# Half-granule signals for the weights' low parts, with three edits to ScalarE's side work and one to a product's order

## What is computed

```
for layer in range(2):                       # hybrid_layer
    p = split_columns(rmsnorm(x, norm_g) @ w_in)
    hm = mlstm_chunkwise(conv+silu(q, k), v, gates)      # 4 heads
    hg = gla_chunked(q, k, v, decays)                    # 4 heads, then rmsnorm by head
    hd = dsa_sparse_attention(q, k, v, index scores, top 128)
    x = x + concat(y_ml, y_gla, y_dsa) @ w_out
u = rmsnorm(x) @ w_in_2                      # second_block
y_a = rwkv7_branch(u)                        # forward and backward scan
y_b = diff_attn_branch(u)                    # 4 heads, 2 softmaxes each
x = x + (gate_a * y_a + gate_b * y_b) @ w_out_2
x = x + relu(rmsnorm(x) @ w_ff1)**2 @ w_ff2
x = x + sigmoid(rmsnorm(x) @ w_ple_gate) * (p @ w_ple_proj)
out = rmsnorm(x)
```

## Time and profile before

| | |
|---|---|
| median of three runs | 2360.22 us |
| the profiled execution's own time | 2368.48 us |
| its span, first to last instruction | 2366.7 us |
| PE busy | 2259.0 us, 95% of the span |
| DVE, ACT, POOL busy | 1202.9, 947.8, 899.2 us |
| idle time of PE that ended with POOL's low part (L346) | 28.5 us in 12 waits |
| granted TensorE clock, mean | 0.987 of 2.4 GHz |

### The profile page before, as it was taken

The page is one execution under the profiler, slowest core; times in us unless marked ns, Lnnn a source line. Parts: engine busy times, 40 slices in busy tenths (PEclk is TensorE's granted clock), DMA queues, the critical chain, the costliest instruction groups (busy, mean ns, idle before and its releaser), DMA issues. The chain is left out here.

```text
span 2366.7 us, 38426 instructions
## 1 busy us (share of the span) xinstructions
PE 2259.0 (95%) x16046; PEld 1750.6 (74%) x16046; DVE 1202.9 (51%) x2014; ACT 947.8 (40%) x1364; POOL 899.2 (38%) x674
## 2 busy tenths in 40 slices
PE   7999999999999999999999988888999999999997
PEld 5776777787877857777778777776666778888885
DVE  5544843334246467343343878853544667307334
ACT  5433355345253224654343433324266333212243
POOL 3342243334443404333344432222332445545543
PEclk9999999999999999999999999998999999999998
DMA  4221222222322212212233200002221233222332
GB/s 148 86 89 36 72 81 71 72 72 76 101 83 78 67 45 85 85 63 80 64 102 104 75 3 4 4 13 83 67 67 54 80 98 98 96 95 94 98 98 71
DMA packets 50568, 175.18 MB, mean 74 GB/s; under 512 B 6036, under 2 KB 7004, under 8 KB 50396
## 3 DMA queue, kind: packets, MB, share of 16 engines
q1 hardware_dynamic: 50396, 172.73, 22.5%
HBM read 170.60 MB, written 2.11 MB: 73 GB/s over the span
## 5 line engine op out<-in xcount | busy, mean ns | idle before, releaser
L346 POOL TENSOR_TENSOR w_low<-work,w_high 128x512 fp32r<-128x512 f32 x614 | 826.5, 1367 | 1215.4 <-ACT w_high L295 1215.4
L276 PE MATMUL ps<-x_high_tiles,w_high 128*128 128x512 f32 x1544 | 626.1, 406 | 28.4 <-POOL w_low L346 20.9
L295 ACT ACTIVATE w_high<-work 128x1024 fp32r<-128x1024 f32 x307 | 325.0, 1058 | 733.8 <-PE ps L276 730.7
L276 PE MATMUL ps<-x_low_tiles,w_high 128*128 128x512 f32 x1544 | 605.1, 392 | 0.8 <-DVE x_low_tiles L369 0.8
L276 PE MATMUL ps<-x_high_tiles,w_low 128*128 128x512 f32 x1544 | 604.6, 392 | 0.0
L276 PE MATMUL ps<-arena_parts,w_high 128*128 128x512 f32 x1264 | 399.7, 393 | 11.3 <-POOL w_low L346 7.2
L276 PEld LDWEIGHTS ps<-x_high_tiles,w_high 128*128 128x128 f32 x1544 | 291.4, 189 | 132.6 <-issue 42.4
L276 PEld LDWEIGHTS ps<-x_low_tiles,w_high 128*128 128x128 f32 x1544 | 291.5, 189 | 64.5 <-DVE x_low_tiles L369 1.6
L276 PEld LDWEIGHTS ps<-x_high_tiles,w_low 128*128 128x128 f32 x1544 | 291.8, 189 | 62.7 <-issue 6.0
L276 PEld LDWEIGHTS ps<-arena_parts,w_high 128*128 128x128 f32 x1264 | 238.8, 189 | 64.3 <-POOL w_low L346 8.6
L276 PE MATMUL ps<-arena_parts,w_low 128*128 128x512 f32 x608 | 237.6, 391 | 0.0
(11 more groups left out here) (454 smaller groups left out, 2903.9 us busy)
## 6 DMA issues: line engine op xcount, KB each, us to landing
work<-w_first SPq DMA_DIRECT2D x178, 512.0 KB, 3.7
work<-w_second SPq DMA_DIRECT2D x134, 512.0 KB, 3.7
xT_sb<-xT SPq DMA_DIRECT2D x8, 256.0 KB, 7.6
outT<-arena SPq DMA_DIRECT2D x8, 256.0 KB, 2.1
arena<-distance_bias SPq DMA_DIRECT2D x4, 256.0 KB
small<-small SPq DMA_DIRECT2D x1, 815.5 KB, 4.6
arena<-consts SPq DMA_DIRECT2D x1, 544.0 KB, 3.7
base<-consts SPq DMA_DIRECT2D x1, 512.0 KB
```

The costliest lines, as they stand in the source:

```text
L276: ins = pe.matmul(out, lhsT, rhs, start=(n == 0 and k == 0 and q == 0), stop=(n == unit["granules"] - 1 and k == len(ops[i]) - 1 and q == 2))
L295: act.activation(m.wh[:, split_of(g), :], m.raw[:, raw_of(g), :], ACT.Copy).then_inc(sem["high_ready"], 1)
L346: ins = pool.tensor_tensor(m.wl[:, split_of(g), part], m.raw[:, raw_of(g), part], m.wh[:, split_of(g), part].bitcast(F32), ALU.subtract)
```

## The change

1. POOL raises `low_ready` after each of its two instructions for a granule instead of after the second alone. PE waits for the first count at the granule's start, and once more before the first tile of the second half of each job's tiles (`second`). SP's waits are for the same events as before, with doubled counts.
2. `renormalise_side`: the high part of the eighth tile is made in the same turn as the other seven.
3. `gla_side`: the four exponentials come one turn after the logarithms.
4. `rwkv_keys_side`: three of the six exponentials come in one turn and three in the next, and the empty turns behind them go from three to one, so that what follows keeps its turn.
5. The first unit of the output product in the last stage goes by tile.

```
                 if g - NRAW >= split:
-                    sp.wait_ge(sem["low_ready"], g - NRAW + 1 - split)
+                    sp.wait_ge(sem["low_ready"], 2 * (g - NRAW + 1 - split))
...
                     if g >= split:
-                        pe.wait_ge(sem["low_ready"], g + 1 - split)
+                        pe.wait_ge(sem["low_ready"], 2 * (g - split) + 1)
...
                     half = len(order) // 2 if len(ops) > 1 else len(order)
+                    second = next(at for at, (i, k) in enumerate(order) if k >= len(ops[i]) // 2)
                     for at, (i, k) in enumerate(order):
                         if at == half:
                             next(beside, DONE)
+                        if at == second and g >= split:
+                            pe.wait_ge(sem["low_ready"], 2 * (g - split) + 2)
...
                 for part in (slice(0, GRAN // 2), slice(GRAN // 2, GRAN)):
-                    ins = pool.tensor_tensor(m.wl[:, split_of(g), part], m.raw[:, raw_of(g), part], m.wh[:, split_of(g), part].bitcast(F32),
-                                             ALU.subtract)
-                ins.then_inc(sem["low_ready"], 1)
+                    pool.tensor_tensor(m.wl[:, split_of(g), part], m.raw[:, raw_of(g), part], m.wh[:, split_of(g), part].bitcast(F32),
+                                       ALU.subtract).then_inc(sem["low_ready"], 1)
...
     def scalar(act, sem):
         yield from turns(at + 3)
         for k in range(KD):
-            if k == KD - 1:
-                yield
             act.wait_ge(sem[done], k + 1)
...
             act.activation(m.gla_rs[:, h, :], AB[h % 2], ACT.Ln, bias=m.eps, scale=1.0 / 128).then_inc(sem["gla_log"], 1)
+        yield
         act.wait_ge(sem["gla_log"], GLA_H)
...
             act.activation(ex, ex, ACT.Exp, scale=-RATE).then_inc(sem["first_exp_ready"], 1)
-        yield from turns(3)
+            yield
+        yield from turns(1)
         for t in range(T):
...
         outs[0]["needs"] = lambda tile: ("dve_evac", 8 + tile + 1)
+        outs[0]["by_tile"] = True
         mixing = cols + branches + outs
```

More of the change, by code:

```diff
@@ L2751, in second_and_next @@
             if keep is None:
-                late = [(at, ("low_ready", 1), *loads[0]), (end - 8, ("gla_out", GLA_H), *loads[1])]
+                late = [(at, ("low_ready", 2), *loads[0]), (end - 8, ("gla_out", GLA_H), *loads[1])]
             else:
-                late = [(at, ("low_ready", 1), *loads[0]), (end - 8, ("gla_out", GLA_H), *loads[1]), (end + 4, ("mm_ready", jobs + KD), *loads[2])]
+                late = [(at, ("low_ready", 2), *loads[0]), (end - 8, ("gla_out", GLA_H), *loads[1]), (end + 4, ("mm_ready", jobs + KD), *loads[2])]
             residual = scaled_side(m, "next", 7, ends, counts, gain, xn, keep=keep, loads=1)
@@ L2781, in build @@
                       norm=[small_in[0][1]], arrive=[small_in[0][0]] + [(m.xT[:, k, :], xT[k, :, :]) for k in range(KD)] + ones, arrivals=arrivals, constants=scalars,
-                      late=[(3, ("low_ready", 1), *load) for load in bias_in] + bounce)
+                      late=[(3, ("low_ready", 2), *load) for load in bias_in] + bounce)
         for layer in range(DEPTH - 1):
@@ L2879, in build @@
                             count(mixing + ffn + projected, "act"), m.c2("norm_final", 8), dst)
-        late = [(3, ("low_ready", 1), *load) for load in rope_in]
+        late = [(3, ("low_ready", 2), *load) for load in rope_in]
         late += [(start + 2, ("mm_ready", branches_done), m.p[:, i, :], pT[i, :, :]) for i in range(2)]
```

3 lines of the change are left out of this document (1 added, 2 removed).

## The result

The changed kernel takes 2347.43 us, the median of six runs (2343.52 to 2352.26); the kernel before, run beside it, takes 2360.8 us (2358.07 to 2364.15). The ratio is 0.9944, with a 95% interval of 0.9928 to 0.9959: 13.4 us less, where 14.25 were forecast (2346.0 us). A second comparison of the same two kernels gave 2348.53 us (2347.11 to 2353.65) beside 2363.35, ratio 0.9945 (0.9932 to 0.9957): 14.8 us by the medians and 13.0 by the ratio. From the kernels that lacked one part each I had expected 15.6 to 16.2 there.

What follows compares the result with a forecast made beforehand. PE, busy 95% of the span, was taken to bound the kernel, so only its idle time and slow stretches could give time. Terms summed to 14.25 us, subtracted from the median 2360.22: 2346.0 us, range 2341 to 2353.

Steps and rivals of the forecast that it cites:

- Start and gates: First granule: PE starts 1.75 us earlier, worth 1.0 us; gates granule in both layers: one wait swapped, -0.1 us in all.
- Output products: Both hybrid layers: PE's 2.42 us stall and the slow stretch behind it go, 4.1 us each, 8.2 us together.
- Projections: Second block: the stage ends 1.04 us earlier and no more, limited by a DVE chain; 1.0 us.
- The +2 of my bounds: Projections of the second block: bounds -1 to +2, for which DVE instructions happen to overlap POOL's.
- Attention: Differential attention: PE gains 1.05 us until its transposes need DVE, repeated at the next head; 2.1 us.
- First branch: First branch product: 1.4 us lost to a later DVE wait, two waits become one, slow stretch follows; -1.55 us.
- Merged product: Merged output product: by tile, PE reaches the last merged tile 2.05 us later, waits 0.45, no slow stretch; 3.6 us.
- Waits: All granules: some 305 more waits on PE, already satisfied ones costing nothing that shows; 0.
- no refund from the clock: Rival: stalls go but slow stretches appear elsewhere as often; three refunds of 1.55 us fall away, 9.6 us, 2350.6; chance 0.15.
- The GLA chain is late: Rival: PE reaches the output product's fourth granule before DVE's first tile, by 1.5 us a layer; 11.3 us, 2348.9; chance 0.09.
- The waits cost: Rival: each of 305 new waits holds PE's queue; change loses from 47 ns, 2380 at 112 ns; chance 0.03.
- absorbed: Rival: DVE and ACT chains beside PE take up the gain, under 4.7 us remain, 2358; chance 0.03.

Runs made afterwards that it cites:

- gla_only: The kernel before with only the GLA exponentials moved one turn later: 2356.91 us beside 2363.35, ratio 0.9971.
- a_only: The kernel before with only the half signals (POOL signals each half, PE waits twice a granule): 2360.21 us beside 2364.46, ratio 0.9985.
- no_split_exps: The changed kernel with all six exponentials of the second block's keys in one turn, as before: 2348.31 us beside 2364.12, ratio 0.9935.
- no_early_tile: The changed kernel with the eighth tile's high part one turn later, as before: 2348.35 us beside 2364.12, ratio 0.9938.
- many_waits: The changed kernel with six more already satisfied waits on PE in each granule: 2346.53 us beside 2363.35, ratio 0.9927.
- before_again: The kernel before, unchanged, run for a second profile: one run of 2363.16 us.
- no_halves: The changed kernel without the half signals (POOL signals and PE waits once a granule): 2355.0 us beside 2364.46, ratio 0.9968.
- no_by_tile: The changed kernel with the first unit of the last stage's output product job by job, as before: 2351.82 us beside 2364.46, ratio 0.9957.
- no_gla_yield: The changed kernel with the four GLA exponentials directly behind the logarithms, as before: 2357.25 us beside 2364.46, ratio 0.9972.
- high_first: The changed kernel with ACT's high part of the weights ahead of two evacuations, before the gates granule: 2345.48 us beside 2363.35, ratio 0.9927.

## Why the prediction was right, point by point

The sum of 14.25 us against measured 13.4 and 14.8 is right, and its largest term, the output products, is right in mechanism and size. That the total is within 1 us is in part luck: the projections and the first branch gave about 1 us each more than forecast, the merged product half a microsecond less and through another wait than the one named. Per term, forecast and what the table of stretches gives:

- **Start and gates: 1.0 and -0.1 us forecast.** Without the half signals A is 135.1, 134.8 and 134.0 us (mean 134.6), with them 133.6: 1.0 us for the start and one gates granule, 0.95 forecast. The three of them scatter by 1.1 us, so this term is known to some tenths only. PE starts 1.7 us earlier behind ACT's high part (4.6 to 2.9 us), and a part is worked off at the slow pace of the start (0.43 us a matmul). At the gates the swap of one wait for two costs 0.1 us a layer (A 133.50 and B 267.22 without it), where 0.05 were forecast.
- **Output products: 2 x 4.1 us forecast.** B gives 3.9 us with its gates granule, forecast 4.05. The cause is the moved exponentials, by gla_only alone. That "the half signal alone would have left about 0.8 us" was true of the third granule (0.75) and false of the product: I had traced DVE's chain only for the whole change, and put a number on the half signal without following what is late next. It changes no term, as both edits came together.
- **Projections: 1.0 us forecast, 2.0 measured.** C is 5.97 us shorter, 3.92 of it the output product's. "The stage can end 1.04 us earlier and no more" is the step that failed in size: DVE does go to its last evacuation without idle time, but the chain itself got shorter too. From its L1638 to that evacuation it took 26.32 us before, 1.04 of them idle, and 24.24 us after (there L1639), so 1.04 us came from the instructions themselves. The +2 of my bounds takes it in, and the traces bear out its reason, which DVE instructions lie beside POOL's. Before (POOL's pair and a DVE instruction beside it) and after (the same DVE instruction, beside none):

```profile
1347.53 3.23 POOL L346 TENSOR_TENSOR w_low<-work,w_high 128x512 fp32r<-128x512 f32 x2 [0.84 <-ACT w_high L295]
...
1349.65 1.65 DVE L1641 TENSOR_TENSOR arena<-arena 128x512 f32<-128x512 f32 x1
```
```profile
1337.17 0.69 DVE L1642 TENSOR_TENSOR arena<-arena 128x512 f32<-128x512 f32 x1
```

  Over the 33 instructions of the chain the excess over their shortest durations is 4.2 us in before and in gla_only, 3.3 in a_only and in no_split_exps, and 3.1 in the changed kernel. So 0.9 us come with the half signals, which shift POOL's pairs along the chain, and 0.1 to 0.2 with the split exponentials. The idle 1.04 us went in gla_only as well, where no half clock followed the stall of 1.98 us.
- **Attention: 2.1 forecast, 2.1 to 2.4 measured.** D is 2.1 us shorter in a_only than in before, with the clock at the same places in both. Up to the first branch's L2393 it is 2.4 us (74.15 to 71.75); the slow stretch behind the merged stall, which fell a little differently, takes 0.3 back.
- **First branch: -1.55 forecast, about -0.3 measured.** This term was wrong, and in its picture too. I had "one wait of about 3.1 us"; there are three, 0.70, 0.68 (for DVE's L2525, which I had not named) and 2.33 us, with matmuls between them. Of the ten profiles with the half signals two show half clock behind them (no_early_tile, many_waits), and it costs 1.6 us there: 0.3 us on the average execution. Of the four without, three show it (before_again, gla_only, no_halves), but there it costs nothing, as the wait for L2497 takes it up. So the first profile of before was the exception in its clock, and the clock made no difference to it.
- **Merged product: 3.6 forecast, 3.05 measured** (no_by_tile against the changed kernel). The slow stretch is gone, as forecast. The wait is 1.4 us less than before instead of 2.05, since the step "PE has 18 matmuls ahead of that wait" looked at the last merged tile alone. By tile, the second job starts after 3 matmuls instead of 12, before the bank that it takes over is free, and waits 1.08 us there; the wait for the last tile is gone. My sign of being right, a wait under 0.6 us, failed. The first profile of before has half clock at this place, the second not, so before gains 2.8 or 1.4 us here by execution.
- **Waits: 0 forecast, 0 measured,** with 1830 more of them in many_waits.
- **Last stage, E: 0.4 us** that I did not forecast; every kernel with the half signals has it and none without. I have not traced it to an instruction.

The terms of the table add up to about 1.0 + 3.9 + 6.0 + 4.5 (D, against the mean of before's two) + 0.4 = 15.8 us, more than the two measured differences. The executions of one kernel scatter by 6 to 10 us, mostly in F and in the mLSTM stretches, so that I can't say whether the 1 to 2.4 us between are more than that.

Of the rivals, *no refund from the clock* comes out wrong at the output products (half clock behind 2.42 us in four of four cases in before, in no kernel with the exponentials moved) and half right as a warning, as the branches show. Its price was wrong as well: 9.6 us drops three refunds and keeps the -1.55 of the first branch, while slow stretches "as often as before" would drop both, which makes 11.15. *The GLA chain is late* did not happen in the changed kernel (0.1 us), and was the whole story in a_only and no_gla_yield. *The waits cost* is out by many_waits and *absorbed*, under 4.7 us in all, by the measured total.

## What to carry to other kernels

A signal at a finer grain moves a wait to the next producer in line: before it is priced, ask at each place who delivers the next operand, and when. The order of jobs is no exception: by tile, the next producer was the bank of the second job. Here the half signals alone gave 4.3 us, the move of four exponentials behind the weights' copy 6.4 us, and with the order by tile (3 us by the trace) and two edits that gave nothing it was 14. An early piece put ahead of a copy that others wait for only swaps waits; by the traces of high_first the copy itself belongs in front. And before building a term on the clock behind one stall, take a second profile of the same kernel: waits repeat to 0.1 us where the clock before them is the same, slow stretches don't.

## What the runs showed of the hardware

- PE's waits for counts already reached cost nothing that shows at a pace of one matmul in 0.2267 us, at eight waits in 24 matmuls (1500 in 340 us; E of 407.46 us with two and with eight).
- Half clock (0.50, 1.2 GHz) behind a stall, over all profiles: behind 2.42 us in 4 of 4; behind 2.48 to 2.49 at the merged product in 4 of 5; behind 2.37 us in 3 of 4; behind 1.98 us in the projections in 3 of 4; behind 0.75 and 2.01 with 5.7 us between them in the first layer twice, in the second never; behind 1.08 us in none of 9. At the gates of no_halves, behind 2.25 us, once in 2. A slow stretch costs 1.4 to 1.7 us (94.5 beside 93.1 us from the first branch's L2393 to the end of D in the two profiles of before; D of 165.1 beside 163.4; 355.1, 356.8 and 358.4 us with none, one and two), where I had worked out 1.55, and nothing where a later wait for another engine takes it up. The Trainium skill, "TensorE: Matmul & The Clock Gate", Part 1, says that the point at which the clock changes varies from run to run, since the chip's look at the activity isn't tied to the kernel. These traces agree: the same waits had half clock behind them in one execution and not in the next.
- DVE's instructions on SBUF can take longer beside POOL's pair: L1641 1.65 us beside it in before and 0.69 beside none in the changed kernel, L1639 (there L1640) 1.76 and 1.78 beside it and 0.68 apart from it. L1580 to L1587, which read PSUM, keep 0.69 and 0.75 us either way.
- The first load of weights releases ACT between 7.10 and 9.26 us after the start of the span, by execution, so the first 2 us of a gain at a kernel's start are not to be read from two profiles.
